# First pair of experts: the picked tokens gathered already transposed, in one fused decoder step

## The reference, cut to what matters

```python
h2 = rmsnorm(x, ffn_norm_w)                      # x * rsqrt(mean(x*x) + eps) * ffn_norm_w
logits = h2 @ w_router + b_router
top_vals, top_idx = lax.top_k(logits, 4);  gates = softmax(top_vals)
# for every expert e, on the tokens that picked it:
u = h2[tokens] @ w_up[e] + b_up[e]               # (rows, 1024) @ (1024, 2048)
a = min(u[0::2], 7) * sigmoid(1.702 * min(u[0::2], 7)) * (clip(u[1::2], -7, 7) + 1)
y[tokens] += gate * (a @ w_down[e] + b_down[e])  # (rows, 1024) @ (1024, 1024)
```

## Time and profile before

| what | value |
|---|---|
| median of 3 runs | 1148.07 us (1147.94 to 1150.03) |
| the profiled execution: span from first to last instruction | 1145.4 us |
| PE busy | 1097.6 us (96%) |
| DVE, ACT, POOL busy | 437.5, 188.0, 88.4 us |
| moved by DMA | 444.36 MB, mean 388 GB/s |
| first pair's `up(0)` starts | 241.25 us |

### The profile page before, as it was taken

How to read it: one execution, slowest core, us unless ns; L and a number is a source line. 1 busy time by engine, 2 the same in 40 slices (tenths; PEclk the granted TensorE clock), 3 DMA queues, 4 the chain that set the end, 5 groups by cost and what they waited for, 6 DMA issues and landing times.

```text
span 1145.4 us, 15065 instructions
## 1 busy us (share of the span) xinstructions
PE 1097.6 (96%) x6055; PEld 497.1 (43%) x6055; DVE 437.5 (38%) x858; ACT 188.0 (16%) x398; POOL 88.4 (8%) x161
## 2 busy tenths in 40 slices
PE   9999999999999999999898999999999999999997
PEld 6689898543333333333333333333333333333332
DVE  4577786753433223233223232323232323232322
ACT  2133341221321101010101010101010101010101
POOL 1785215000000000000000000000000000000000
PEclk9999999999999999999999999999999999999999
DMA  9947629999999999999999999999999999999997
GB/s 313 314 128 186 210 85 353 416 357 425 400 420 426 419 432 431 430 433 431 433 433 429 434 430 433 435 428 434 429 434 431 431 434 429 435 429 434 425 423 287
DMA packets 53206, 444.36 MB, mean 388 GB/s; under 512 B 13101, under 2 KB 19373, under 8 KB 35741
## 3 DMA queue, kind: packets, MB, share of 16 engines
q1 hardware_dynamic: 46712, 435.83, 91.7%
q0 software_dynamic: 5600, 7.32, 2.4%
q10 hardware_dynamic: 852, 0.64, 0.2%
HBM read 439.78 MB, written 2.37 MB: 386 GB/s over the span
## 4 chain that ended last, share of the span: by engine, by line
PE 62%; DMA 37%; DVE 0%; issue 0%; ACT 0%; ACTq 0%; SPq 0%; DVEq 0%
PE pA L2051 32%; PE pB L2051 21%; DMA ring<-in_w_up 21%; DMA ring<-in_w_down 10%; PE pM L2051 6%; DMA area<-in_w_up 5%; PE pM L2054 1%; PE pA L2054 1%; DMA x<-in_x_prompt 1%; ACT area L1269 0%; DVE x L1898 0%; SPq L800 0%; DVE conv_row L1812 0%; DVE area L1973 0%; DVE x L1978 0%
## 5 line engine op out<-in xcount | busy, mean ns | idle before, releaser
L2051 PE MATMUL pA<-ring,hn 128*64 128x512 f32 x1536 | 352.6, 602 | 23.0 <-DMA ring<-in_w_up 23.0
L2051 PEld LDWEIGHTS pA<-ring,hn 128*64 128x64 f32 x1536 | 105.3, 137 | 218.8 <-issue 185.5
L2051 PE MATMUL pB<-ring,area 128*64 128x512 f32 (+2 forms) x784 | 171.5, 591 | 6.6 <-DMA ring<-in_w_down 5.8
L2051 PE MATMUL pA<-area,hn 128*64 128x512 f32 x512 | 119.3, 610 | 10.4 <-DMA area<-in_w_up 10.4
L2051 PE MATMUL pB<-area,ring 128*128 128x132 f32 (+2 forms) x928 | 126.4, 327 | 0.0
L2051 PEld LDWEIGHTS pB<-area,ring 128*128 128x128 f32 (+1 forms) x928 | 106.7, 175 | 18.2 <-issue 2.3
L2051 PEld LDWEIGHTS pB<-ring,area 128*64 128x64 f32 (+2 forms) x784 | 58.5, 136 | 101.2 <-issue 87.8
L1898 DVE TENSOR_TENSOR x<-pM,x 128x512 f32<-128x512 f32 x60 | 40.1, 691 | 147.7 <-PE pM L2051 147.7
L1257 ACT ACTIVATE area<-area 128x512 f32<-128x512 f32 x30 | 18.9, 631 | 385.2 <-DVE area L1881 385.2
L1812 DVE COPY conv_row<-pM 128x512 f32<-128x512 f32 x30 | 20.6, 686 | 146.0 <-PE pM L2051 146.0
L2051 PEld LDWEIGHTS pA<-area,hn 128*64 128x64 f32 x512 | 36.2, 139 | 74.5 <-issue 59.7
(11 more groups left out here) (348 smaller groups left out, 907.1 us busy)
## 6 DMA issues: line engine op xcount, KB each, us to landing
ring<-in_w_up SPq DMA_DIRECT2D x36, 4096.0 KB, 29.8
ring<-in_w_down SPq DMA_DIRECT2D x18, 4096.0 KB, 29.0
area<-in_w_up SPq DMA_DIRECT2D x12, 4096.0 KB, 30.2
ring<-in_w_up SPq DMA_DIRECT2D x16, 2048.0 KB, 13.4
area<-in_w_down SPq DMA_DIRECT2D x6, 4096.0 KB, 30.0
ring<-in_w_in SPq DMA_DIRECT2D x22, 1024.0 KB, 10.0
ring<-in_w_down SPq DMA_DIRECT2D x16, 1024.0 KB, 11.6
ring<-in_w_up SPq DMA_DIRECT2D x16, 1024.0 KB, 8.4
```

What stands on the lines that cost most here:

```text
L2051: return pe.matmul(out, w, m, start=start, stop=stop, skip_group_check=True)
```

## The change

In the first pair's gather the operands change places: x (every fourth column, 128 of them) and `s_parts` become stationary and the pick matrix moves, so that PSUM receives the picked tokens transposed. DVE multiplies these pieces by `ffn_norm_w` straight into `xsT`. The copies to `xrow` on DVE and ACT, the eight transposes and their four PSUM fills are gone. The products with the second half of the prompt (`last_columns`) stand ahead of `up(0)` for pieces 0 and 1, and ahead of `up(1)` for pieces 2 and 3; `up(0)` to `up(3)` wait for `xs_ready`, which DVE raises.

```diff
--- before.py
+++ after.py
@@ -277,7 +277,7 @@
             "v_rows": 0, "k_rows": 0, "state_cols": 0, "cache_cols": 0, "conv_rows": 0,
             "s_split": 0, "part": 0, "ahead": 0, "gather": 0, "s_scores": 2, "q_norm": 2}
 FILL, _n = {}, 0
-for _s in STEPS + BRANCH + [("x_turn", n) for n in range(4)]:
+for _s in STEPS + BRANCH:
     _n += FILLS_OF.get(_s[0], 1)
     FILL[_s] = _n
 PRE_FILLS = _n
@@ -637,8 +637,7 @@
         s_pick_ready = sem("s_pick_ready")
         first_pick = sem("first_pick")
         first_full = sem("first_full")
-        first_rows = sem("first_rows")
-        first_rows_act = sem("first_rows_act")
+        xs_ready = sem("xs_ready")
         total_over = sem("total_over")
         flag_ready = sem("flag_ready")
         s_parts_ready = sem("s_parts_ready")
@@ -1228,11 +1227,6 @@
                 act.wait_ge(ex_in, n + 1)
                 nc.scalar.activation(gate[0:r, a, :], lg[0:r, a, :], ACT.Exp,
                                      bias=stat[0:r, 52 + a:53 + a]).then_inc(ex_out, 1)
-
-            for n in (1, 3):
-                act.wait_ge(first_full, n + 1)
-                f = slice(256 * n, 256 * n + 256)
-                nc.scalar.activation(xrow[:, f], first_xs(n), ACT.Copy).then_inc(first_rows_act, 1)
 
             def hn_split(n):
 
@@ -1815,15 +1809,11 @@
                 return V.tensor_tensor(xsT[:, 4 * half:4 * half + 4, :], b.rearrange("p (k s) -> p k s", k=4),
                                        fw[:, 4 * half:4 * half + 4, :], ALU.mult)
 
-            for n in (0, 2):
+            dve.wait_ge(fnorm_loaded, 16)
+            for n in range(4):
                 dve.wait_ge(first_full, n + 1)
-                f = slice(256 * n, 256 * n + 256)
-                V.tensor_copy(xrow[:, f], first_xs(n)).then_inc(first_rows, 1)
-                if n == 0:
-                    dve.wait_ge(fnorm_loaded, 16)
-                for k in (n, n + 1):
-                    V.tensor_tensor(xsT[:, 2 * k:2 * k + 2, :], misc_bank()[:, 0:256].rearrange("p (k s) -> p k s", k=2),
-                                    fw[:, 2 * k:2 * k + 2, :], ALU.mult).then_inc(misc_free, 1)
+                V.tensor_tensor(xsT[:, 2 * n:2 * n + 2, :], first_xs(n).rearrange("p (k s) -> p k s", k=2),
+                                fw[:, 2 * n:2 * n + 2, :], ALU.mult).then_inc(xs_ready, 1)
 
             def picks(to, place):
 
@@ -2311,14 +2301,6 @@
                                 start=(k == 0), stop=(k == KT - 1))
                 return mm
 
-            def piece(t, n):
-
-                f = t[:, 512 * (n // 2):512 * (n // 2) + 512].rearrange("p (i r) -> p i r", r=ROWS)
-                return f[:, :, 2 * (n % 2):2 * (n % 2) + 2]
-
-            def first_out(n):
-                return first_xs(n).rearrange("p (i r) -> p i r", r=2)
-
             def columns_of(w, a, n):
 
                 w = w.rearrange("p (g a c) -> p g a c", a=2, c=2 * ROWS)
@@ -2334,8 +2316,16 @@
                     for a in range(2):
                         matmul(up_out(e, a, n), sel[0:96, e, :], columns_of(bias_up[0:96], a, n), start=start, stop=False)
 
+            def first_columns(n, rows_, chosen, start=False, stop=False):
+
+                for k in (2 * n, 2 * n + 1):
+                    f = rows_[:, 512 * (k // ROWS) + k % ROWS:512 * (k // ROWS) + 512:ROWS]
+                    mm = matmul(first_xs(n)[:, 128 * (k % 2):128 * (k % 2) + 128], f, chosen,
+                                start=(start and k % 2 == 0), stop=stop)
+                return mm
+
             def first_gather(n):
-                return matmul(first_out(n), gathers[0], piece(x[:, 0, :], n), stop=False)
+                return first_columns(n, x[:, 0, :], gathers[0], start=True)
 
             for what, a in BRANCH:
                 if what == "out":
@@ -2414,8 +2404,7 @@
                     pe.wait_ge(s_parts_ready, 1)
                     pe.wait_ge(s_pick_ready, 1)
                     for n in range(4):
-                        matmul(first_out(n), s_pick[0:96].rearrange("p e s -> p (e s)"),
-                               piece(s_parts[0:96], n), start=False, stop=False)
+                        first_columns(n, s_parts[0:96], s_pick[0:96].rearrange("p e s -> p (e s)"))
                 elif what == "count":
                     b = misc_bank()
                     if a == 0:
@@ -2437,23 +2426,13 @@
                 mm.then_inc(misc_full, 1)
 
             pe.wait_ge(first_pick, 2)
-            def first_turn(n):
-
-                b = misc_bank()
-                if n % 2:
-                    pe.wait_ge(first_rows_act, n // 2 + 1)
-                else:
-                    pe.wait_ge(first_rows, n // 2 + 1)
-                for k in range(2):
-                    mm = tr(b[:, 128 * k:128 * k + 128], xrow[:, 256 * n + k:256 * n + 256:2])
-                mm.then_inc(misc_full, 1)
-
-            for n in range(4):
-                matmul(first_out(n), gathers[1], piece(x[:, 1, :], n),
-                       start=False).then_inc(first_full, 1)
-                if n:
-                    if n < 3:
-                        first_turn(n - 1)
+            def last_columns(n):
+
+                first_columns(n, x[:, 1, :], gathers[1], stop=True).then_inc(first_full, 1)
+
+            last_columns(0)
+            last_columns(1)
+
             def gather(b, half, freed=False, parts=True):
 
                 f = slice(512 * half, 512 * half + 512)
@@ -2521,9 +2500,9 @@
                     c = j % UP_CHUNKS
                     if first and e == 0:
                         if c == 1:
-                            first_turn(2)
-                            first_turn(3)
-                        pe.wait_ge(misc_free, FILL["x_turn", c])
+                            last_columns(2)
+                            last_columns(3)
+                        pe.wait_ge(xs_ready, c + 1)
                     elif j in (0, 2):
                         pe.wait_ge(misc_free, base - 1 + j // 2 - (1 if pair1 else 0))
                     w = loaded(j)
```

## The result

| kernel | median | lowest to highest | runs |
|---|---|---|---|
| before | 1148.01 us | 1147.28 to 1150.03 | 6 |
| after | 1151.85 us | 1150.44 to 1152.34 | 6 |

The ratio is 1.003, with a 95% interval from 1.0021 to 1.004: the change makes the kernel slower by 0.3%. The prediction (1147.1, no more than 1148.9) has the wrong sign. The profiled execution took 1152.3 us, with a span of 1150.5.

The account below looks back on a forecast made before the run. PE was taken to set the pace until about 505 us, DMA behind it. Terms of +0.06, -1.53 and +0.48 made -0.99 us at `up(1)`, hence 1147.1 us for 1148.07, range 1146.2 to 1148.9.

Parts of the forecast that it names:

- What bounds the kernel: Whole kernel: PE sets the pace until about 505 us, DMA behind; PE's shift at 382 moves the end equally.
- Hidden: Rival, chance 0.18: DMA makes up the bytes missing at 242 later, so the end does not move, 1148.1 us.
- Refills decide: Rival, chance 0.10: only the dry DMA stretch at 242 counts, so the end moves by 1.47 us, to 1146.6.
- The pace of the new passes: First pair's gather: each 128-column pass with its own stationary load takes 0.12 us, where old 256-column passes took about 0.23.
- the far end: Gather passes at 0.235 us, load and streaming added up: 1150.3 us, left outside the range.
- up to the count: Three pieces of the first prompt half ahead of the count: 1.59 us for 1.53, +0.06 on the path.
- piece 3: Between the count and 238.38: this piece +0.02, samples the same 0.46 us, hidden by 0.26 us of slack, so 0.
- from the pick matrix to `up(0)`: Second pick matrix to `up(0)`: turns and copies go, `up(0)` starts at 239.72 for 241.25, -1.53 us.
- from `up(0)` to `up(1)`: Ahead of `up(1)`: eight gather passes, 1.15 us, replace turns of 0.67, giving back +0.48.
- The new wait for DVE: Ahead of `up(0)`: PE finishes piece 1 at 239.45, then idles some 0.27 us until DVE's multiplication is done.
- Loads that don't hide: Rival, chance 0.11: loads add to streaming, 0.235 us a pass over 32 float32 passes, +2.2 us, 1150.3; anywhere from 1148.1 up.
- The sum: All terms together: `up(0)` -1.47 us, `up(1)` and all later PE work -0.99, giving 1147.1 us.

Follow-up runs that it names:

- Step four behind `up(0)` only: The change with neighbouring columns as stationary operands everywhere except the eight passes ahead of `up(1)`, which keep every fourth column: 1148.13 us, 0.9996 of the kernel before.
- step eight: The change with every eighth column as stationary operand on all pieces, in place of every fourth: 1153.02 us, one run.
- the runs of step one: The change with neighbouring columns, first-pair upward weights and norm weights read to match: 1146.62 us (0.9993 of before), again 1147.5 (0.9996).

## Why the prediction was wrong

**What bounds the kernel** held. PE's shift at `up(1)` reaches the end through the places of the ring: +3.04 there, +3.28 at the last weights, and the table above shows the same for eleven other profiles. So *Hidden* falls for a loss, which was not absorbed; for a gain of 1 us the runs are too close to no change. *Refills decide* does not fit the change itself, whose refills come 1.65 later and whose last weights land 3.28 later. Step four behind `up(0)` only tests it, by one profile: its refills come as early as in the four profiles with neighbouring columns of x and no step four in float32, but its last weights land 0.47 to 1.26 us later than theirs, as its `up(1)` does (0.5 to 1.26). That speaks against it; the times of the runs (0.9996 of before, with neighbouring columns 0.9992) don't tell the two apart.

**The pace of the new passes** is the step that failed. 0.12 us was taken from two rows, each of which has half of what the new passes have: a two-pass float32 product with neighbouring columns, and a one-pass transpose with a step of four. That both agree said nothing on the two together, which cost 0.233 (neighbouring columns 0.112, step two 0.118, step eight 0.238; the transpose with step four 0.12). The prediction wrote that the trace has no such product, and kept 0.235 as the far end. That end has the right size by another mechanism: it added a load of 0.12 and the stream in series, but the stream is hidden, and the loads themselves follow each other at 0.23 us. Why a two-pass load should pay for the step and a one-pass load not, no run here shows.

**The other terms**, with a pass at 0.233 and the clock as it was:

| term | forecast | measured |
|---|---|---|
| up to the count: three pieces | +0.06 | +1.55 (234.60 to 237.68, for 1.53) |
| bias product and count | 0 | +0.45 (237.68 to 238.88, for 0.75), at the lower clock |
| piece 3 (238.88 to 239.95, for 0.53) and samples with the wait behind (0.86 for 0.72) | 0 | +0.54, +0.14 |
| from the pick matrix to `up(0)` (240.81 to 242.90, for 2.87) | -1.53 | -0.78 |
| from `up(0)` to `up(1)` (5.86, for 4.47) | +0.48 | +1.39 |
| `up(1)` | -0.99 | +3.29 |

The measured terms add up to 3.29. The new wait for DVE did not end last: DVE took up the first piece at 242.14 for 0.42 us, and PE was in its own passes of piece 1 until `up(0)` at 242.90.

```profile
242.14 0.42 DVE L1815 TENSOR_TENSOR hn<-pB,fnorm 128x256 f32<-128x256 f32 x1 [2.06 <-PE pB L2041]
```

The slack ahead of the second pick matrix was used up, as the second rival had it.

**Loads that don't hide** gave +2.2 at `up(1)`, and +1.40 ahead of it. Measured is 13.24 - 10.87 = +2.37 with step eight, where the clock did not fall, and +1.39 ahead of `up(1)` in after. Its size was right and its reason was not. The rest of the 3.29, about 0.9, is the lower clock, which no case had.

**The sum is right where a pass does take 0.11.** With neighbouring columns `up(0)` comes 1.53 earlier than before, counted from the first gather pass (forecast 1.47), and `up(1)` 1.11 (forecast 0.99), with PE idle for 0.19 us in the new wait (forecast 0.27). That shows the other terms right, and that the one price decided the sign. Even so the end would have moved by about 1 us, which the runs of step one cannot tell from no change.

## What to carry to other kernels

A float32 product that takes its stationary operand with a step of four or eight elements paid 0.23 us for each load of 128 x 128 here, twice that of step one or two, so before operands change places, look at which of them is strided and lay the data out (here: the rows of the weights) so that the stationary one is not. Two rows that each share one property with a new operation do not price the operation that has both: where they are all there is, the far end deserves a real chance. Where PE hands out a ring's places, a shift at the last point ahead of the steady stream reached the end nearly one for one here (3.04 there, 3.28 at the last weights), so that point is the one to cost.

## What the runs showed of the hardware that was not expected

- The load's step: 0.112, 0.118, 0.233 and 0.238 us a pass for steps of one, two, four and eight; one-pass transposes (0.12) and bfloat16 products (0.39 us for four passes) with step four at no extra price.
- The granted clock fell to 0.5 behind passes that the load paces, though the profile shows PE busy all the time: for 6.8 us in one profile of the change, 3.4 in the other, and not at all with step eight. It cost about 0.9 us.
- The last stores take a different time from run to run: two stores of `out` in SP's queue are 1.19 us long in the profile of before and 2.08 in after, which is 0.9 of the 1.8 us by which the spans differ beyond the shift. SP's timeline (start, us, what) at the end of before, then of after:

```profile
1140.54 1.19 SPq L933 DMA_DIRECT2D out<-x  x2
```

```profile
1143.81 2.08 SPq L932 DMA_DIRECT2D out<-x  x2
```
